# The up projection of a gated ConvFFN by seven block products of sums in place of eight, with the gated tiles kept in memory

## What is computed

```python
h = rms_norm(x, norm_ffn_pre_w)
up = causal_dwconv(h @ ffn_w_up, ffn_conv_w, ffn_conv_b)   # 1024 -> 2 x 2816, width 3
gate, val = _split(up, (FFN_D_FF, FFN_D_FF))
ff = (jax.nn.gelu(gate, approximate=True) * val) @ ffn_w_down
return x + rms_norm(ff, norm_ffn_post_w)
```

## Time and profile before

| | |
|---|---|
| median of 3 runs | 2241.0 us (2239.64 to 2245.46) |
| the profiled execution | 2241.06 us, span 2239.5 us |
| mean granted TensorE clock | 0.983 |
| busy: PE, DVE, ACT, POOL | 96%, 57%, 33%, 21% of the span |
| up projection | from about 1494 to 1975 us |
| down projection | from about 1975 us to the end |

### The profile page before, as it was taken

How to read it: one execution, slowest core, us unless ns; L and a number is a source line. 1 busy time by engine, 2 the same in 40 slices (tenths; PEclk the granted TensorE clock), 3 DMA queues, 4 the chain that set the end, 5 groups by cost and what they waited for, 6 DMA issues and landing times. The chain is left out here.

```text
span 2239.5 us, 28556 instructions
## 1 busy us (share of the span) xinstructions
PE 2150.1 (96%) x10502; PEld 1791.2 (80%) x10502; DVE 1282.1 (57%) x1601; ACT 738.7 (33%) x1382; POOL 465.1 (21%) x486
## 2 busy tenths in 40 slices
PE   7999999979989989989979999999999999999997
PEld 7888889958878868878758888888888888888885
DVE  6855553149989989989843444544333334352532
ACT  5322221014444444444442223333222222243432
POOL 1000011146656556566410000000000000000000
PEclk9999999989999999999989999999999999999999
DMA  6132352233343343333264433221111111133353
GB/s 220 63 97 79 102 169 87 77 100 112 110 145 119 103 134 115 110 106 111 79 226 151 145 141 118 104 85 47 52 51 47 47 47 47 43 125 92 103 159 89
DMA packets 125913, 232.72 MB, mean 104 GB/s; under 512 B 24784, under 2 KB 69968, under 8 KB 125808
## 3 DMA queue, kind: packets, MB, share of 16 engines
q1 hardware_dynamic: 82560, 163.97, 23.3%
q0 software_dynamic: 13040, 46.41, 6.1%
q10 hardware_dynamic: 30208, 20.98, 2.9%
HBM read 178.62 MB, written 52.69 MB: 103 GB/s over the span
## 5 line engine op out<-in xcount | busy, mean ns | idle before, releaser
L153 PE MATMUL lt_ps<-lt_h_hi,lt_w_hi 128*128 128x512 f32 x1216 | 476.1, 392 | 16.5 <-DVE lt_h_lo L1775 14.3
L154 PE MATMUL lt_ps<-lt_h_lo,lt_w_hi 128*128 128x512 f32 x1216 | 474.0, 390 | 0.0
L155 PE MATMUL lt_ps<-lt_h_hi,lt_w_lo 128*128 128x512 f32 x1216 | 473.9, 390 | 0.0
L153 PEld LDWEIGHTS lt_ps<-lt_h_hi,lt_w_hi 128*128 128x128 f32 x1216 | 228.8, 188 | 65.4 <-issue 15.0
L155 PEld LDWEIGHTS lt_ps<-lt_h_hi,lt_w_lo 128*128 128x128 f32 x1216 | 228.7, 188 | 48.0
L154 PEld LDWEIGHTS lt_ps<-lt_h_lo,lt_w_hi 128*128 128x128 f32 x1216 | 228.8, 188 | 46.8
L1727 DVE SCALAR_TENSOR_TENSOR lt_xc<-lt_ps,lt_cw,lt_xc 128x1023 f32<-128x1023 f32 x44 | 56.5, 1284 | 270.7 <-ACT lt_xc L1543 270.7
L153 PE MATMUL ps_zg<-u_hi,g_hi 128*128 128x512 f32 x448 | 185.7, 415 | 0.0
L155 PE MATMUL ps_zg<-u_hi,g_lo 128*128 128x512 f32 x448 | 176.7, 394 | 0.0
L154 PE MATMUL ps_zg<-u_lo,g_hi 128*128 128x512 f32 x448 | 175.1, 391 | 0.0
L1543 ACT ACTIVATE lt_xc<-lt_ps,lt_cw 128x1024 f32<-128x1024 f32 x44 | 53.1, 1207 | 302.5 <-PE lt_ps L155 302.5
(11 more groups left out here) (280 smaller groups left out, 4333.6 us busy)
## 6 DMA issues: line engine op xcount, KB each, us to landing
lt_w_raw<-in_w_up SPq DMA_DIRECT2D x44, 512.0 KB, 3.4
mx_a_row<-acs_s SPq DMA_DIRECT2D x32, 512.0 KB, 3.9
g_raw<-in_w_xbc SPq DMA_DIRECT2D x24, 512.0 KB, 3.5
tok_s<-fr_work POOLq DMA_DIRECT2D x24, 512.0 KB, 3.9
lt_sig<-gate_s SPq DMA_DIRECT2D x24, 512.0 KB, 3.7
lt_w_raw<-in_w_down SPq DMA_DIRECT2D x32, 384.0 KB, 3.1
lt_w_raw<-in_w_down SPq DMA_DIRECT2D x32, 320.0 KB, 2.9
g_raw<-in_w_gate SPq DMA_DIRECT2D x16, 512.0 KB, 4.9
```

The lines of the kernel that those rows point to most:

```text
L153: pe.matmul(dst, s_hi, m_hi, start=first, stop=False)
L154: pe.matmul(dst, s_hi, m_lo, start=False, stop=False)
L155: return pe.matmul(dst, s_lo, m_hi, start=False, stop=last)
```

## The change

A pair is now computed as a product of 2 x 2 blocks: the reduction in halves of 4 tiles (LO, HI), the two column blocks of the pair, the two halves of 512 tokens. a11, a12, a22 are blocks of h, b11 to b22 of the weights (11 and 21 from the value block `raw_a`, 12 and 22 from the gate block `raw_b`). s1 to s4 are sums of blocks of h, made once; t1 to t4 are sums of blocks of weights, made for each pair. Seven products P1 to P7, in the order P1, P5, P6, P2, P7, P3, P4, each of 4 x 3 matmuls of 512 columns into a bank of its own (P4 shares P6's), replace eight. Pair 0 keeps the eight.

- POOL makes s2 and s4 per token tile (`sums`), t1 to t4 per pair (`weight_sums`), and two combines in SBUF, u4 and c22 (`u4_c22`).
- ACT copies P1 and P5 to SBUF and makes seven hi copies of 512 elements per pair in place of two of 1024; its taps read SBUF.
- DVE makes seven lo splits of 512, five combines of a PSUM bank and an SBUF tile (u2, c11, u3, c12, c21), and the convolution from SBUF (`up_a`, `up_b`).
- For token tiles 0 to 3 ACT keeps a copy of h (`h0`); for tiles 4 to 7 `split_h` makes s3 (LO of the second tokens less LO of the first) and s1 from the transposed tile and splits two halves, four DVE operations in place of one.
- The sums take ff's place in SBUF. Each gated tile `fo` is stored to `ff_s` in memory by SP, and POOL loads the halves back: the first half in six transfers, each when a product of the last pair has used a tile for the last time (`FIRST`), the second half (`SECOND`) when the last tile is gated, with the residuals behind it.
- The order of the last pair and of the splits for the down projection is written anew on ACT and DVE. The down projection itself is as before.

The core of the diff:

```diff
+        a11 = h_hi[:, LO, 0:HALF], h_lo[:, LO, 0:HALF]
+        a12 = h_hi[:, HI, 0:HALF], h_lo[:, HI, 0:HALF]
+        a22 = h_hi[:, HI, HALF:SEQ], h_lo[:, HI, HALF:SEQ]
+        s3 = h_hi[:, LO, HALF:SEQ], h_lo[:, LO, HALF:SEQ]
+        s1, s2, s4 = (s1_hi, s1_lo), (s2_hi, s2_lo), (s4_hi, s4_lo)
+
+        b11, b21 = (a_hi[:, LO], a_lo[:, LO]), (a_hi[:, HI], a_lo[:, HI])
+        b12, b22 = (b_hi[:, LO], b_lo[:, LO]), (b_hi[:, HI], b_lo[:, HI])
+        t1, t2, t3, t4 = ((t_hi[:, n], t_lo[:, n]) for n in range(4))
+        raw_b, raw_a = w_raw[:, 0], w_raw[:, 1]
+
+        OPS = ((b11, raw_a[:, LO], 1, 0), (t1, t_f[:, 0], 2, 1), (t2, t_f[:, 1], 3, 3), (b21, raw_a[:, HI], 4, 0),
+               (t3, t_f[:, 2], 5, 2), (b22, raw_b[:, HI], 6, 0), (t4, t_f[:, 3], 7, 4))
...
+        FIRST = ((0, h_f[:, 1, LO, 0:HALF], 1), (4, s1_f[:], 2), (8, s2_f[:], 3), (12, h_f[:, 1, HI, 0:HALF], 4),
+                 (16, h_f[:, 1, LO, HALF:SEQ], 5), (20, s4_f[:, 0:1], 6))
+        SECOND = ((0, st_b[:]), (4, h_f[:, 0, HI, HALF:SEQ]), (8, h_f[:, 1, HI, HALF:SEQ]), (12, st_u[:]), (18, st_s[:]),
+                  (20, st_r[:]))
...
+            def load_pair(i):
+
+                sp.wait_ge(op_lo_done, N_OPS * i - (2 * N_OPS - 4))
+                sp.wait_ge(t_ready, N_SUMS * i - N_SUMS)
+                load_a(i)
+                sp.wait_ge(op_lo_done, N_OPS * i - (2 * N_OPS - 6))
+                load_b(i)
+
+            def store_ff(i):
+                sp.wait_ge(ff_done, i + 1)
+                sp.dma_start(ff_s[bass.ds(i, 1)].rearrange("a p n -> p (a n)"), fo[:]).then_inc(ff_stored, 16)
...
+            def weight_sums(i):
+                pool.wait_ge(a_in, 16 * i + 16)
+                pool.wait_ge(b_in, 16 * i + 16)
+                pool.tensor_tensor(t_f[:, 0], raw_b[:, LO], raw_a[:, LO], ALU.subtract).then_inc(t_ready, 1)
+                pool.tensor_tensor(t_f[:, 2], raw_b[:, LO], raw_b[:, HI], ALU.subtract).then_inc(t_ready, 1)
+                pool.wait_ge(t_ready, N_SUMS * i - (N_SUMS - 1))
+                pool.tensor_tensor(t_f[:, 1], raw_b[:, HI], t_f[:, 0], ALU.subtract).then_inc(t_ready, 1)
+                pool.wait_ge(t_ready, N_SUMS * i - 1)
+                pool.tensor_tensor(t_f[:, 3], raw_a[:, HI], t_f[:, 1], ALU.subtract).then_inc(t_ready, 1)
+
+            def u4_c22(i):
+                pool.wait_ge(u2_ready, i)
+                pool.wait_ge(p5_kept, i)
+                pool.tensor_tensor(u4[:], u2[:], p5[:], ALU.add).then_inc(u4_ready, 1)
+                pool.wait_ge(u3_ready, i)
+                pool.wait_ge(conv_b_done, i)
+                pool.tensor_tensor(up_b[:, HALF:SEQ], u3[:], p5[:], ALU.add).then_inc(c22_done, 1)
...
+            weight_sums(1)
+            with pool.Fori(1, LAST) as i:
+                pool.wait_ge(op_lo_done, N_OPS * i)
+                weight_sums(i + 1)
+                u4_c22(i)
+            for g, (k, place, n) in enumerate(FIRST):
+                if g == 5:
+                    u4_c22(LAST)
+                pool.wait_ge(product_done, N_PRODUCTS * (LAST - 1) + n)
+                pool.wait_ge(ff_stored, 16 * min(k + 4, LAST))
+                pool.dma_start(place, ff_s[k:k + place.shape[1], :, 0:HALF].rearrange("k p n -> p k n")).then_inc(f_in[g], 16)
+            pool.wait_ge(product_done, N_PRODUCTS * LAST)
+            pool.wait_ge(ff_done, FT)
+            for g, (k, place) in enumerate(SECOND):
+                pool.dma_start(place, ff_s[k:k + place.shape[1], :, HALF:SEQ].rearrange("k p n -> p k n")).then_inc(g_in[g], 16)
...
+                if t < TH:
+                    act.activation(h0[:, :, c], ps_t[:], ACT.Copy).then_inc(h0_done, 1)
+                    act.activation(h_hi[:, :, c], ps_t[:], ACT.Copy).then_inc(h_hi_done, 1)
+                else:
+                    act.activation(s1_f[:, :, (t - TH) * P:(t - TH + 1) * P], ps_t[:, HI], ACT.Copy).then_inc(a22_kept, 1)
+                    act.activation(h_hi[:, HI, c], ps_t[:, HI], ACT.Copy).then_inc(h_hi_done, 1)
+                    act.wait_ge(s3_ready, t - TH + 1)
+                    act.activation(h_hi[:, LO, c], h_f[:, 1, LO, c], ACT.Copy).then_inc(s3_hi_done, 1)
...
+            def pair(i, second):
+                keep_p1(i)
+                tap_a(i - 1, second)
+                gelu(i - 1)
+                keep_p5(i)
+                for n in range(6):
+                    split_op(n, i + 1, False)
+                tap_b(i, False)
+                split_op(6, i + 1, False)
...
+                dve.tensor_tensor(h_f[:, 1, LO, c], ps_t[:, LO], h0[:, LO, e], ALU.subtract).then_inc(s3_ready, 1)
+                dve.wait_ge(a22_kept, n)
+                dve.tensor_tensor(s1_f[:, :, e], ps_t[:, LO], s1_f[:, :, e], ALU.add).then_inc(s1_ready, 1)
                 dve.wait_ge(h_hi_done, t + 1)
-                dve.tensor_tensor(h_lo[:, :, t * P:(t + 1) * P], ps_t[:], h_hi[:, :, t * P:(t + 1) * P].bitcast(F32),
-                                  ALU.subtract).then_inc(h_lo_done, 1)
-
-            def split_up(i, j):
-                dve.wait_ge(w_hi_done, 2 * i + (MERGE + j + 1))
-                dve.tensor_tensor(w_lo[:, j], w_raw[:, j], w_hi[:, j].bitcast(F32), ALU.subtract).then_inc(w_lo_done, 1)
+                dve.tensor_tensor(h_lo[:, HI, c], ps_t[:, HI], h_hi[:, HI, c].bitcast(F32), ALU.subtract).then_inc(h_lo_done, 1)
+                dve.wait_ge(s3_hi_done, n)
+                dve.tensor_tensor(h_lo[:, LO, c], h_f[:, 1, LO, c], h_hi[:, LO, c].bitcast(F32), ALU.subtract).then_inc(s3_lo_done, 1)
...
+                conv_a(i - 1)
+                split_op(0, i + 1)
+                gated(i - 1, second)
+                split_op(1, i + 1)
+                u2_of(i)
+                split_op(2, i + 1)
+                c11(i)
+                split_op(3, i + 1)
+                u3_of(i)
+                split_op(4, i + 1)
+                c12(i)
+                split_op(5, i + 1)
+                conv_b(i)
+                c21(i)
+                split_op(6, i + 1)
...
+            dve.wait_ge(s4_ready, TH)
+            split_sum(1, s1_lo, s1_f[:], s1_hi)
+            split_sum(2, s2_lo, h0[:, LO], s2_hi)
+            split_sum(3, s4_lo, h0[:, HI], s4_hi)
...
+            i = LAST
+            conv_a(i - 1)
+            gated(i - 1, False)
+            u2_of(i)
+            c11(i)
+            split_down(0)
+            u3_of(i)
+            for k in range(4):
                 split_ff(0, k)
-            conv(i, 0)
-            split_down(0)
             split_down(1)
-            for k in range(5, 8):
+            c12(i)
+            conv_b(i)
+            for k in range(4, 8):
+                split_ff(0, k)
+            c21(i)
+            conv_a(i)
+            gated(i, False)
+            for k in range(8, 12):
                 split_ff(0, k)
             split_down(2)
-            for k in range(8, 11):
-                split_ff(0, k)
             split_down(3)
-            conv(i, 1)
-            for k in range(11, 13):
+            for k in range(12, LAST):
                 split_ff(0, k)
             split_down(4)
-            gated(i)
-            for k in range(13, 17):
-                split_ff(0, k)
+            split_ff(0, LAST)
             split_down(5)
...
+                product(ps_p1, b11, a11, True, True).then_inc(product_done, 1)
...
+                op(2)
+                if second:
+                    pe.wait_ge(sum_lo_done, 2)
+                    pe.wait_ge(c11_done, 1)
+                else:
+                    pe.wait_ge(c21_done, i)
+                product(ps_p6, t2, s2, True, True).then_inc(product_done, 1)
...
+                op(6)
+                pe.wait_ge(u2_ready, i)
+                product(ps_p4, t4, a22, True, True).then_inc(product_done, 1)
...
+            pair(1, True)
+            with pe.Fori(2, FT) as i:
+                pair(i, False)
 
             for q in range(2 * PAIRS):
+                if q == 0:
+                    pe.wait_ge(u3_ready, LAST)
+                    pe.wait_ge(c12_done, FT)
```

509 lines of the change are left out of this document (357 added, 152 removed).

## The result

| | before | after |
|---|---|---|
| median | 2241.4 us (2239.6 to 2245.5, 4 runs) | 2228.9 us (2226.2 to 2229.7, 4 runs) |
| ratio, 95% interval | | 0.994, 0.9922 to 0.9957 |
| span of the profiled execution | 2239.5 us | 2226.5 us |

The account below looks back on a forecast made before the run. TensorE was taken as the bound: -57.1 for 252 matmuls, +3.4 way in, +0.8, +6.5, +2.7 and +2.5 way out, sum -41.2 us, from 2241.0 to 2200 us. Own range 2192 to 2211; stated range with rivals 2190 to 2232.

Parts of the forecast that it names:

- ff 4, weight block 2: Start of the down projection: TensorE waits for DVE's splits of ff 4 (+0.8 us) and weight block 2 (+6.5 us).
- post row ahead of block 6: Down projection: DVE waits for the post row, loaded behind a backlog, before splitting block 6; +2.5 us, bounds 0 and 12.
- clock behind the stops: Down projection: after the long stop TensorE runs some 5.4 us at the lower clock level; +2.7 us.
- DVE's new period: Up projection loop: DVE's turn walked to 18.5 us, under TensorE's 19.04, so +0 for 20 pairs.
- The ring: The loop's walk of one turn through DVE, POOL additions and ACT's taps, back to its start; 18.5 us claimed.
- The exclusive part: Loop: of each POOL addition's 1.04 us, 0.90 was counted as shutting out DVE operations with two SBUF inputs.
- (a): Rival: loop bound by DVE and POOL, 19.3 to 21.0 us a turn, say 20.1; 2222 us, chance 0.20.
- The way in: Last transposes to the loop's first pairs: TensorE waits as DVE's splits come late; +3.4 us, bounds 1 and 8.
- The way out: Last pair into the down projection: waits of +0.8, +6.5 and +2.5 us, and +2.7 for the clock.
- (b): Rival: POOL and DVE never overlap in the loop, 21.3 us a turn; 2247 us, slower than before, chance 0.08.
- (c): Rival: longer way out, a weight load starves or ff's first half lands late, +12 to +15; 2214 us, chance 0.12.
- (d): Rival: the seven products each leave a bubble on TensorE in the loop, +15; 2215 us, chance 0.05.

Follow-up runs that it names:

- e5: Against after: DVE's wait for the post row moved from ahead of the down loop to the first product using it; 2225.3 us, ratio to before 0.9943.
- e6: Against after: in the last pair, weight blocks 2 and 3 and gated tiles 8 to 11 split ahead of conv a, block 4 ahead of the gating; 2225.8 us.
- e8: e5, e6 and e7 together, with c12 of the last pair behind gated tile 1's split; 2196.4 us, ratio to before 0.9814.
- e4: Against after: POOL's four weight sums made on 8 of 512 elements a partition, for timing alone (wrong output); 2206.4 us, turn 19.04.
- e7: Against after: c21 ahead of conv b, and split 6 ahead of tap b on ACT and conv b on DVE; 2207.9 us, turn 19.04.
- e9: Against after: the four weight sums of each later pair made by DVE instead of POOL; 2216.3 us, turn 19.61.
- e1: Against after: c21 put ahead of conv b on DVE in the loop, nothing else moved; 2211.5 us, turn 19.27.
- e2: Against after: P4 given a bank of its own, so the next pair's P6 no longer waits for c21; 2229.5 us, ratio to before 0.9944.
- e10: Against e8: pair 1's splits 0 and 1, gated tiles 4 and 5 and weight block 5 split earlier, POOL's late loads held back; 2189.7 us.
- e3: Against after: c22 added on DVE right behind u3 instead of on POOL; 2230.7 us, turn 20.38.

## Why the prediction was wrong in size

| term | predicted | measured in the traces |
|---|---|---|
| 252 matmuls | -57.1 | -57.1 |
| loop above its floor, P3 of pair 1 to P3 of pair 21 | 0 | 405.8 - 20 x 19.04 = +25.0 |
| wait at the last transposes | +0.7 | +1.2 |
| rest of the way in | +2.7 | +2.9 |
| c12 of the last pair, ahead of down | 0 | +2.0 |
| ff 4, weight block 2 | +0.8, +6.5 | +1.5, +6.5 |
| post row ahead of block 6 | +2.5 | +3.65 |
| clock behind the stops | +2.7 | +4.1 |
| stages ahead of the change | 0 | -2.7 |
| sum, from span 2239.5 | -41.2 | -13.0 |

The measured rows: from the transposes' start to the first down matmul 471.7 us before, 444.5 after; way out 264.7 and 280.5. "Rest of the way in" and "clock" are what the other lines leave of these two. The predicted 2.7 of "rest of the way in" holds 0.9 for pairs 1 and 2, which are measured in the line of the loop: its first turn took 21.17, the other nineteen 20.25, so 0.9 of the 25.0 is the way in.

**The step that failed is "DVE's new period"**, the walk that ended at 18.5 us a turn and so put the loop at TensorE's floor, "+0 for 20 pairs"; the turn measured 20.25, and that makes 24 of the 28 us missed. The ring it describes is the right one; three of its numbers were low, and between them made 1.75:

- The two idle times. I took 1.9 from a combine to DVE's next step, so 0.7 idle; it is 1607.86 - 1605.42 = 2.44, so 1.15. ACT's tap on SBUF takes 1.24, not the 1.06 of the gelu, and 0.32 pass between the combine's end and the tap. Twice 0.45: **+0.9**.
- The exclusive part, 0.90 each. One that falls on a split or on the gating costs DVE 1.10; conv a's two steps paid 0.19 and 0.81. u4 and c22 cost 0.50 each, because a combine, which reads PSUM, covers the rest: no combine in the turn shown was lengthened, as the walk had it. 4.2 in place of 3.5: **+0.7**.
- DVE's own work 13.75 in place of 13.6: **+0.15**. By starts it is the 13.6 of the walk; the rest is the 0.08 by which the last operation ahead of each idle time outlasts its 0.60.

18.5 + 1.75 = 20.25; the third number is what the turn leaves, so the sum closes by construction. Also 1.04 for an addition came from one with an operand broadcast; two different operands take 1.30 with nothing in the way. The slack of 0.5 us a turn between 18.5 and 19.04 was thinner than the walk's own error, and that should have given rival (a) more than 0.20. (a) is what happened: 20.1 foreseen, 20.25 measured, 2222 against 2228.9. Of the 6 us between the sums, 3 are the loop's; the way out has 5 more and the stages ahead take 2.7 back.

The Trainium skill, SBUF — State Buffer, "Who interferes with whom", holds that the two engines lock each other out for the whole instruction. The prediction weighed it and took less. The traces agree in the main: 1.10 on split 0 and on the gating, most of an addition's 1.30, and 2.78 for two additions in a row.

**The way in** was right in kind and 1.6 short: 1.2 + 2.9 and the 0.9 of pair 2 make 5.0 where 3.4 were forecast, mainly since split 0 was late by 3.0 in place of 1.8. **The way out** was right in kind at each place: block 2 at 6.5, the post row's wait, both behind the splits foreseen. Two things were missing. c12 comes behind four gated tiles' splits; on the walk these took the 2.49 of the earlier trace rows, but u4 and c22 stretched them to 5.25, so TensorE stopped for 2.0 before down. And the second stop cost clock too. TensorE behind its two stops, and a window behind each (columns as above):

```profile
1961.41 0.80 PE L154 MATMUL lt_ps<-lt_s_hi,lt_d_hi 128*128 128x512 f32 x1 [6.54 <-DVE lt_d_lo L2013]
...
1983.21 0.80 PE L154 MATMUL lt_ps<-lt_h_hi,lt_d_hi 128*128 128x512 f32 x1 [3.65 <-DVE lt_d_lo L2013]
```

```profile
1962.00:1964.00 2.00, 2.00 (x6) 1.61 (x5) 2.00 (x5) 1.77 (x4) 2.00 (x4) 0.50 1.01 399
1984.00:1986.00 2.00, 2.00 (x7) 1.52 (x6) 0.00 (x0) 0.00 (x0) 0.00 (x0) 0.50 0.88 261
```

After 3.65 us without a matmul the clock is 0.50, its lower level (1.2 GHz), as after 6.54; I had charged it only once. The wait for the post row, on DVE, counted from P3's end near 1941.2: the row was issued at 1973.7, that is at 32.5 in place of 29, and took 8.6 us in place of 7.4. From 1974 to 1982 SP's queue moved 1.18 MB, 0.15 a us: more than the 0.11 of the prediction, less than the 0.2 that it worked out for equal turns.

```profile
1982.33 1.56 DVE L2013 TENSOR_TENSOR lt_d_lo<-lt_w_raw,lt_d_hi 128x640 fp32r<-128x640 f32 x2 [9.05 <-DMA lt_f_post<-in_ffn_post_row]
```

**Rivals.** (b) is out: combines run beside POOL undisturbed, and the turn was below 21. (c) did not occur in after: e5 shows that at block 6 the weights were there. It was near, though: as soon as TensorE came to block 6 earlier, the weights were late (e6, e8). (d) is out: at 19.04 a turn (e4, e7) seven products leave no bubble.

## What to carry to other kernels

An elementwise operation moved from VectorE to GpSimd isn't free to VectorE when both read two SBUF operands: here four additions cost VectorE 3.2 us a turn (up to 1.10 each) where it does them in 0.60 each, so moving them back made the loop faster (e9). When an engine newly gets to 80 or 90% busy, look for a ring through it: follow each engine's order once round, count the idle times at handovers, and put operations that are already ready into them (e1 and e7: 1.2 us a turn for reordering alone). A wait's name on the bound engine tells where the delay arrives, not where it arises: it changed in e2, in e6 and at the way in of e10, and the time there did not, or hardly.

## What the runs showed that was not expected

A GpSimd addition's duration follows the VectorE operation that it meets: 1.30 alone, 1.67 beside splits of 512, 2.28 beside operations of 1024, and 3.34 beside a split of 2048. POOL and DVE at the way in of after, a weight sum and the split of a sum of h:

```profile
1508.36 3.34 POOL L1618 TENSOR_TENSOR lt_t_f<-lt_w_raw 128x512 f32<-128x512 f32 x1
```

```profile
1507.18 3.37 DVE L1942 TENSOR_TENSOR lt_s_lo<-lt_s_f,lt_s_hi 128x2048 fp32r<-128x2048 f32 x1 [0.59 <-POOL lt_h L1612]
```

3.34 = 1.30 and 2.04, which is about the 2.28 that a split of 2048 takes by itself (e10, 1519.59), less what had run. So each seems to wait for the other's whole instruction, and short VectorE operations let GpSimd in soonest. That no operation is split between the two is read from these durations only; no run tried other full widths on POOL.

The clock did not follow the length of a stop alone. A stop of 1.2 us a turn didn't lower it in the loop of after (1.00 over fifteen turns), and one of 3.65 did. But the same stop of 3.0 us for split 0 of pair 1 was followed by the full clock in after (1.00 from 1519 to 1523), e2, e3, e4, e6, e7 and e9, and by the lower one in e1, e5 and e8; here e1, behind its stop that ended at 1521.74:

```profile
1524.00:1525.00 1.00, 1.00 (x4) 0.80 (x3) 1.00 (x3) 0.19 (x1) 0.00 (x0) 0.50 0.31 74
```

The stop of 2.0 us ahead of down had the full clock behind it in after (1.00 from 1946 to 1949) and mostly the lower one in e5 (0.55 from 1948 to 1951). What decides it, no run here shows: a stop of 2 to 3 us cost clock in one trace and not in another.
